# Expert 0 by its own 64 rows, the full sort behind it, one weight piece in the sorted rows' place and nine rotating buffers: a hybrid mixer and mixture-of-experts kernel

## The reference

```python
h = rmsnorm(x, norm1_g);  u = h @ w_in                     # 2048 -> 5632 columns
x = x + concat([conv(u_a), attention(u_q, u_k, u_v), conformer(u_c)]) @ w_out
h = rmsnorm(x, norm2_g)
pg = softmax(h @ rg_w + rg_b); grp = argmax(pg)            # 4 groups
le = (h @ re_w + re_b)[grp]                                # 8 experts in a group
q_top, e_top = top_k(softmax(le), 2)                       # 2 experts for each token
y[t] = sum over the 2 experts e:  gate * (silu(h[t] @ w_gate[e]) * (h[t] @ w_up[e])) @ w_down[e]
out = rmsnorm(x + y, final_g)
```

## Time and profile before

| | before |
|---|---|
| median of 3 runs | 1361.73 us |
| the profiled execution's own time | 1361.14 us |
| its span, first to last instruction | 1359.3 us |
| PE busy | 1235.7 us (91%) |
| DVE, ACT busy | 511.2, 280.0 us |
| DMA over the span | 471.8 MB, 347 GB/s |
| chain that ended last, by engine | PE 55%, DMA 40%, DVE 2% |

### The profile page before, as it was taken

One profiled execution on the slowest core, in us unless ns is written; L12 is line 12 of the kernel. 1 busy time (PEld: TensorE's weight loads), 2 busy tenths in 40 slices (PEclk: granted clock), 3 DMA queues, 4 the chain that ended last, 5 costly groups with the idle time before them and its releaser, 6 DMA issues.

```text
span 1359.3 us, 16672 instructions
## 1 busy us (share of the span) xinstructions
PE 1235.7 (91%) x6468; PEld 682.4 (50%) x6468; DVE 511.2 (38%) x906; ACT 280.0 (21%) x383; POOL 6.0 (0%) x27
## 2 busy tenths in 40 slices
PE   5999999989989999989899888989898989898896
PEld 5999999978866333333333333333333333333332
DVE  5365868655437422322222222222222222222224
ACT  5443444436343100100001000000100000100002
POOL 1000000000000000000000000000000000000000
PEclk9999999989999999999999999999999999999998
DMA  8555354547466999999999999999999999999994
GB/s 274 203 181 191 128 184 155 185 155 278 148 265 245 427 427 427 429 427 428 429 429 428 429 428 429 430 427 430 428 428 429 429 428 429 428 428 429 427 423 165
DMA packets 63443, 471.80 MB, mean 347 GB/s; under 512 B 5895, under 2 KB 6407, under 8 KB 37676
## 3 DMA queue, kind: packets, MB, share of 16 engines
q1 hardware_dynamic: 63404, 471.24, 84.5%
HBM read 469.13 MB, written 2.10 MB: 347 GB/s over the span
## 4 chain that ended last, share of the span: by engine, by line
PE 55%; DMA 40%; DVE 2%; issue 2%; ACT 1%; SPq 0%; DVEq 0%; ACTq 0%
DMA ring<-in_w_up 39%; PE bank L1301 24%; PE bank L1468 15%; PE bank L1503 8%; PE bank L1516 3%; PE bank L1445 1%; PE bank L1469 1%; DMA stage<-in_w_in 1%; PE bank L1485 1%; PE bank L1411 1%; PE bank L1478 0%; DVE x_tok L1174 0%; DVE zone_u L859 0%; ACT w_hi L354 0%; PE bank L1378 0%
## 5 line engine op out<-in xcount | busy, mean ns | idle before, releaser
L1468 PE MATMUL bank<-ring,win 128*64 128x512 f32 x992 | 442.9, 600 | 64.4 <-DMA ring<-in_w_up 64.4
L1469 PE MATMUL bank<-ring,win 128*64 128x512 f32 x992 | 443.8, 601 | 0.0
L1468 PEld LDWEIGHTS bank<-ring,win 128*64 128x64 f32 x992 | 132.3, 138 | 350.4 <-issue 315.8
L1174 DVE TENSOR_TENSOR x_tok<-x_tok,bank 128x512 f32<-128x512 f32 x256 | 158.7, 682 | 264.0 <-PE bank L1516 263.1
L1503 PE MATMUL bank<-ring,hiddenT 128*64 128x512 f32 x1024 | 226.8, 594 | 18.2 <-issue 17.5
L360 DVE TENSOR_TENSOR w_lo<-stage,w_hi 128x2048 fp32r<-128x2048 f32 x60 | 137.3, 2295 | 94.5 <-ACT w_hi L354 94.2
L1301 PE MATMUL bank<-h_hi,w_hi 128*128 128x256 f32 x576 | 163.7, 284 | 1.5 <-DVE w_lo L360 1.5
L1301 PE MATMUL bank<-h_lo,w_hi 128*128 128x256 f32 x576 | 163.3, 283 | 0.0
L1301 PE MATMUL bank<-h_hi,w_lo 128*128 128x256 f32 x576 | 163.3, 283 | 0.0
L1503 PEld LDWEIGHTS bank<-ring,hiddenT 128*64 128x64 f32 x1024 | 84.4, 137 | 136.7 <-issue 115.9
L354 ACT ACTIVATE w_hi<-stage 128x2048 fp32r<-128x2048 f32 x60 | 114.8, 1917 | 144.1 <-PE bank L1301 140.2
(11 more groups left out here) (222 smaller groups left out, 839.0 us busy)
## 6 DMA issues: line engine op xcount, KB each, us to landing
ring<-in_w_gate SPq DMA_DIRECT2D x62, 2048.0 KB, 27.0
ring<-in_w_up SPq DMA_DIRECT2D x62, 2048.0 KB, 31.1
ring<-in_w_down SPq DMA_DIRECT2D x62, 2048.0 KB, 27.1
stage<-in_w_in SPq DMA_DIRECT2D x44, 1024.0 KB, 4.9
stage<-in_w_out SPq DMA_DIRECT2D x16, 1024.0 KB, 5.1
ring<-in_w_up SPq DMA_DIRECT2D x4, 1024.0 KB, 16.8
ring<-in_w_gate SPq DMA_DIRECT2D x4, 1024.0 KB, 16.5
ring<-in_w_down SPq DMA_DIRECT2D x4, 1024.0 KB, 27.9
```

The lines of the kernel that those rows point to most:

```text
L1174: V.tensor_tensor(at, at, bank[banks[n]][:, :], ALU.add).then_inc(returned, 1)
L1468: M.matmul(bank[0][0:W_ROWS, :], rows_of[:, c, 0:W_ROWS], gate[:, at], start=(c == 0), stop=(c == C - 1))
L1469: ins = M.matmul(bank[0][UPPER, :], rows_of[:, c, 0:W_ROWS], up[:, at], start=(c == 0), stop=(c == C - 1))
```

## The change

1. The ring has nine buffers: seven from the start, the other two in the memory of y_hi and y_lo. Rounds are of three experts. silu_g and hidden share one tile, and final_w gets no memory of its own: it is loaded into ring buffer 7 after everything else.
2. Piece 2 goes to `zone_piece`, the first 4096 columns of zone_u, where x_sorted will stand later. So pieces 0 to 7 are issued before expert 0 is begun; piece 2 follows the loads of the third block of w_out.
3. ScalarE copies each block of x_tok into x_cols, channels regrouped (`columns_out`), two copies of 128x512 a block.
4. Expert 0's 64 rows come from a product of their own, x_cols with first_pick (a mask of 64 slots scaled by the norm), plain fp32, 32 matmuls of 64 columns; VectorE applies g2 and writes win.
5. h2_hi and h2_lo are made in four parts each from x_cols.
6. The sort is of all 512 slots, 16 chunks: chunks 0 to 2 before down(0), 3 to 15 behind it. Six banks rotate. ScalarE empties odd chunks, VectorE even ones. Expert 1's window waits for all.
7. SP's waits follow: pieces 8 and 9 after two quarters of expert 0, 10 after four, 11 and 12 behind down(0)'s halves, 13 and 14 behind half the sort and all of it (their memory held h2), 15 and 16 behind half of expert 1.

```diff
-RING = 8
-LATE = 7
-LATE_FROM = 4
-ROUND = 4
+RING = 9
+EARLY = 7
+FIRST_LOADS = EARLY + 1
+ZONE_PIECE = 2
+TURN = (0, 1, 2, 3, 4, 7, 8, 5, 6)
+ROUND = 3
 PIECE = C * NB // 2
 PART = PIECE // 2
-SORT = SLOTS // 2
+HC = C // 2
...
-        xT = u3(T * D, T, NB)
+        zone_piece = zone_u[:, 0:PIECE]
+        x_cols = u3(PIECE, T, D).rearrange("p t (c k) -> p t c k", c=C)
...
-        silu_g = sb("silu_g", [P, NB])
-        hidden = sb("hidden", [W_ROWS, NB])
+        rows_now = sb("rows_now", [P, NB])
+        silu_g, hidden = rows_now[W_ROWS:, :], rows_now[0:W_ROWS, :]
+        sq_out = (x_sorted_spare, rows_now[:, :])
+        win_t = sb("win", [P, C * W_ROWS])
+        win = win_t[:, :].rearrange("p (c n) -> p c n", c=C)
+        xT = win_t[:, :].rearrange("p (t n) -> p t n", t=T)
+        first_pick = sb("first_pick", [P, T, W_ROWS])
...
+        ring += [sb(f"ring{k}", [P, PIECE]) for k in range(EARLY, RING)]
+        final_w = ring[EARLY][:, 0:D]
...
+            assert n != ZONE_PIECE
+            if n < FIRST_LOADS:
+                return n - (n > ZONE_PIECE), 16
+            turn, at = divmod(n - FIRST_LOADS, RING)
+            slot = TURN[at]
+            return slot, 16 * (turn + 1 + (slot < EARLY))
...
-        SORT_BANK, SORT2_BANK = (0, 1, 2, 3, 6, 4, 5, 7), (1, 2, 3, 4, 5, 6, 7, 1)
+        WIN_BANK, SORT_BANK = (1, 2, 3, 6), (1, 3, 6, 7, 0, 2)
...
+                if b == 2:
+
+                    sp.wait_ge(yc_ready, J)
+                    sp.dma_start(zone_piece, first[gate_last]).then_inc(zone_loaded, 16)
...
+            load_piece(slot_of(0, up_last), first[up_last])
             sp.wait_ge(lo_made, chunk(LAST_OUT + 3))
-            load_piece(3, first_pieces[3])
+            load_piece(slot_of(0, down_first), first[down_first])
             sp.wait_ge(used, chunk(LAST_OUT + 2))
-            load_piece(4, first_pieces[4])
+            load_piece(slot_of(0, down_last), first[down_last])
             sp.wait_ge(used, chunk(LAST_OUT + 3))
-            load_piece(5, first_pieces[5])
-
-            gate_first, up_first, gate_last, up_last, down_first, down_last = range(PIECES)
-            second = expert_pieces(1)
             load_piece(slot_of(1, gate_first), second[gate_first])
-            for h in range(2):
-                for k, part in ((up_first, HALF[h]), (gate_last, HALF[h])):
-                    sp.wait_ge(in_used, h + 1)
-                    slot = slot_of(1, k)
-                    sp.dma_start(ring[slot][:, part], second[k][:, part]).then_inc(piece_loaded[slot], 16)
+            load_piece(slot_of(1, up_first), second[up_first])
...
+            sp.wait_ge(in_used, 2)
+            load_piece(slot_of(1, gate_last), second[gate_last])
+            load_piece(slot_of(1, up_last), second[up_last])
             sp.wait_ge(in_used, QUARTERS)
-            load_piece(slot_of(1, up_last), second[up_last])
             load_piece(slot_of(1, down_first), second[down_first])
-            sp.wait_ge(sorted2_done, 8)
+            sp.wait_ge(down_used, 2)
             load_piece(slot_of(1, down_last), second[down_last])
-            third = expert_pieces(2)
-            sp.wait_ge(down_used, 2)
+            sp.wait_ge(down_used, J)
             load_piece(slot_of(2, gate_first), third[gate_first])
-            sp.wait_ge(down_used, J)
+            sp.wait_ge(sorted_done, HC)
             load_piece(slot_of(2, up_first), third[up_first])
+            sp.wait_ge(sorted_done, C)
+            load_piece(slot_of(2, gate_last), third[gate_last])
             sp.wait_ge(in_used, QUARTERS + 2)
-            load_piece(slot_of(2, gate_last), third[gate_last])
-            for k in (up_last, down_first, down_last):
-                load_next(2, k, slot_of(2, k), third)
-            sp.dma_start(final_w[:, :], a["final_g"].rearrange("(o d) -> o d", o=1).broadcast_to([P, D])).then_inc(fg_loaded, 16)
-            fourth = expert_pieces(3)
-            for k in range(PIECES):
-                load_next(3, k, slot_of(3, k), fourth)
+            load_piece(slot_of(2, up_last), third[up_last])
+            load_piece(slot_of(2, down_first), third[down_first])
+            load_next(2, down_last, slot_of(2, down_last), third)
...
+            sp.dma_start(final_w, a["final_g"].rearrange("(o d) -> o d", o=1).broadcast_to([P, D])).then_inc(fg_loaded, 16)
...
+            def columns_out(b):
+
+                for t in range(T):
+                    act.wait_ge(mixed_added, 2 * b + t + 1)
+                    nc.scalar.activation(x_cols[:, t, :, b * NB // C:(b + 1) * NB // C],
+                                         x_tok[:, t, b * NB:(b + 1) * NB].rearrange("p (k c) -> p c k", c=C),
+                                         ACT.Copy).then_inc(x_cols_made, 1)
...
+            columns_out(BLOCKS - 1)
+            act.wait_ge(h_ready, T + 1)
+            act.wait_ge(used, chunk(4 * MOE_BLOCK0 - 1))
+            act.wait_ge(x_cols_made, T * BLOCKS)
+            for half in range(2):
+                for t in range(T):
+                    nc.scalar.activation(h2_half(0, t, half), x_cols[:, t, half * HC:(half + 1) * HC].rearrange("p c k -> p (c k)"),
+                                         ACT.Copy, scale=RSTD[:, t:t + 1]).then_inc(h2_hi_made, 1)
...
+            def sort_out(c):
+
+                act.wait_ge(sorted_done, c + 1)
+                nc.scalar.activation(x_sorted[:, c, :], bank[SORT_BANK[c % len(SORT_BANK)]][:, :], ACT.Copy,
+                                     scale=g2[:, c:c + 1]).then_inc(sorted_act, 1)
...
+            sort_out(1)
             act.wait_ge(down_used, J)
             nc.scalar.activation(y_rows[:, 0:NB], bank[4][:, :], ACT.Copy).then_inc(y_act, 1)
+            for c in range(3, C, 2):
+                sort_out(c)
+            act.wait_ge(starts_ready, 1)
+            act.wait_ge(sorted_act, HC)
+            act.wait_ge(sorted_dve, HC)
+            window(1)
...
+            V.tensor_tensor(FIRST_SLOT, SLOT[:, 0:T], SLOT[:, T:2 * T], ALU.min).then_inc(slot_first, 1)
+            dve.wait_ge(slot_first, 1)
+            for t in range(T):
+                V.tensor_scalar(first_pick[:, t, :], iota_row[:, 0:W_ROWS], FIRST_SLOT[:, t:t + 1], RSTD[:, t:t + 1],
+                                ALU.is_equal, ALU.mult).then_inc(first_picked, 1)
...
+            for i in range(C // WIN_C):
+                cs = slice(i * WIN_C, (i + 1) * WIN_C)
+                dve.wait_ge(first_rows, i + 1)
+                V.tensor_tensor(win[:, cs, :], bank[WIN_BANK[i]][:, 0:WIN_C * W_ROWS].rearrange("p (c n) -> p c n", c=WIN_C),
+                                g2[:, cs].unsqueeze(2).broadcast_to([P, WIN_C, W_ROWS]), ALU.mult).then_inc(first_win, 1)
...
+            for half in range(2):
+                for t in range(T):
+                    dve.wait_ge(h2_hi_made, T * half + t + 1)
+                    V.scalar_tensor_tensor(h2_half(1, t, half), x_cols[:, t, half * HC:(half + 1) * HC].rearrange("p c k -> p (c k)"),
+                                           RSTD[:, t:t + 1], h2_half(0, t, half).bitcast(F32),
+                                           ALU.mult, ALU.subtract).then_inc(h2_lo_made, 1)
...
+            crowded(0)
+            hidden_made(0)
+            sort_out(0)
+            hidden_back(0)
+            sort_out(2)
+            for i in range(1, 4):
                 crowded(i)
-            hidden_made(0)
-            for i in range(0, 8, 2):
-                evicted(sorted2_done, SECOND, SORT2_BANK, i, sorted2_dve)
-            hidden_back(0)
-            for i in range(OVER // 2, OVER):
+            upper_rows(0)
+            for c in range(4, C, 2):
+                sort_out(c)
+                if c in (6, 10):
+                    crowded(4 + (c == 10))
+            for i in range(6, OVER):
                 crowded(i)
             crowded_tables()
...
+            pe.wait_ge(x_cols_made, T * BLOCKS)
+            for t in range(T):
+                pe.wait_ge(first_picked, t + 1)
+            for c in range(C):
+                at = c % WIN_C * W_ROWS
                 for t in range(T):
-                    if p == 0:
-                        pe.wait_ge(pick_ready, t + 1)
-                        pe.wait_ge(h2_hi_made, t + 1)
-                    else:
-                        pe.wait_ge(h2_lo_made, t + 1)
-                    for i, b in enumerate(SORT_BANK):
-                        if p == 0 and t == 0 and b in (4, 5, 7):
-                            pe.wait_ge(places_saved, T + 1)
-                        for k in range(2):
-                            ins = sorted_from(bank[b][:, k * SORT:(k + 1) * SORT], part, t, 2 * i + k, slice(0, SORT),
-                                              p == 0 and t == 0 and k == 0, p == 1 and t == T - 1 and k == 1)
-                        if p == 1 and t == T - 1:
-                            ins.then_inc(sorted_done, 1)
+                    ins = M.matmul(bank[WIN_BANK[c // WIN_C]][:, at:at + W_ROWS], x_cols[:, t, c, :], first_pick[:, t, :],
```

(33 more changed lines are left out.)

## The result

The changed kernel takes 1366.49 us (median of 6 runs, 1365.47 to 1368.87), the kernel before 1361.27 in the runs beside it: ratio 1.0039, 95% interval [1.0029, 1.0049]. That is slower by 5.2 us. The prediction was 1367.6 with a range of 1360.0 to 1369.8. The profiled run took 1365.47 us with a span of 1363.7, 4.3 and 4.4 us over those of before.

The account below looks back on a forecast made before the run. From 424 us the weight stream was taken to bound the kernel. TensorE's steps from 407.6 summed to X = 470.4; X - 463.9 gave +6.5 us on the profiled 1361.14, so 1367.6, range 1360.0 to 1369.8.

Parts of the forecast that it names:

- first rival: Expert 0's 64-row product: the clock rises inside it, so it ends at 417.3; change +0.5 us, 1361.6; chance 27%.
- X: Moment when TensorE is half through expert 1 and SP can issue piece 15, the stream's last stop; forecast 470.4.
- Start of the product: Expert 0's new 64-row product on TensorE starts at about 407.6, where the sort started at 407.70.
- The product: Expert 0's 64 fp32 records on TensorE: 6.9 us at full clock, 13.7 at low; low taken, ending at 421.3.
- Gate and up: Expert 0's gate and up products: 13.9 us at full clock plus 2.0 for a cold start, done at 437.2.
- Turns, three chunks, down(0): Expert 0 behind gate and up: turns 1.0, three sorted chunks of 0.92, down 6.9; sum 10.7 us, to 447.9.
- Thirteen chunks: Rest of the sort behind down(0): 13 chunks of 0.92 us, 11.9, to 459.8, with evictions keeping up.
- Eviction, register, window: Between sort and expert 1: last eviction 0.8, ScalarE's register read 0.75, window 1.1, 0.1 to TensorE; to 462.5.
- Half of expert 1: Half of expert 1's gate and up: 7.1 us, plus 0.8 taken for the clock behind 2.7 us of idleness.
- form of the sum: Weight stream after its last stop: 4.92 us a piece before and after, so the change in time is X - 463.9.
- X - 463.9: Change in total time from X, at 4.92 us a piece of the weight stream; +6.5 us forecast.
- second hole: Weight stream between pieces 14 and 15: 0 GB/s for about 5 us, from 465.6 to 471.

Follow-up runs that it names:

- after_twice: Changed kernel with each of the 64-row product's 64 records issued once more, its result overwritten: 1379.10 us, ratio 1.0132 to the kernel before.
- after_128cols: Changed kernel with expert 0's product made 128 columns wide, the window taking the first 64: 1362.27 us, ratio 1.0004 to the kernel before.
- after_high_only: Changed kernel with expert 0's rows made from the high halves alone (fp32r, 32 records instead of 64): 1361.33 us, ratio 0.9998 to the kernel before.
- after_warm: Changed kernel with filling products, never read, in TensorE's waits around the routing to keep the clock up: 1359.77 us, ratio 0.999 to the kernel before.
- before_final_last: Kernel before with only the final norm's weights moved, issued behind the last expert's pieces: 1358.38 us, ratio 0.9982 to the kernel before.
- after_warm3b: Second run of the changed kernel with filling products around the routing, ahead of expert 1 and in the layer norm's idle stretch: 1354.75 us, ratio 0.9953.
- after_warm3: Changed kernel with filling products around the routing, ahead of expert 1 and ten in the layer norm's idle stretch: 1355.66 us, ratio 0.9959 to the kernel before.

## Why the prediction was right

The mechanism was the one predicted, and its steps can be read off one by one. The stated range alone would not have shown it, as it held the first rival's 1361.6 too; the product's 0.50 and the moment X do.

- *Start of the product:* 408.20 against 407.6; the routing ran 0.35 us later in this run, and the wait for the slots is 1.65.
- *The product:* 64 records at the low clock, 13.7 us expected, 13.8 from its start to expert 0's first product at 422.02. The choice between 6.9 and 13.7, the largest in the sum, fell right, but the reason given for it holds only in part. That the 40-column records were the nearer kind is borne out: behind the narrow records the clock did not rise in 27.5 us (after_twice). But their pace, which I put down to weight loads, is not what tells them apart: records of 128 columns keep the same pace, and behind 5.4 us of those it rose (after_128cols).
- *Gate and up:* 422.02 to 436.92, 14.9 us, of which 1.0 is the cold start; 2.0 was expected. The clock came back about 2 us into it (0.94 over 424 to 425), and not 4.
- *Turns, three chunks, down(0):* 436.92 to 447.91, 11.0 against 10.7. VectorE's gates were done at 432.9 (432.30 and 0.60), so it was hidden by 4 us and not 1.7: it made the low halves from contiguous rows, 4.9 us in two pairs, where I had taken the strided 7.56 of the earlier trace rows.
- *Thirteen chunks:* 12.0 against 11.9. The evictions kept up, 0.69 us on ScalarE and 0.75 on VectorE.
- *Eviction, register, window:* to 462.8, against 462.5.
- *Half of expert 1:* 7.1, and nothing for the idle stretch where I took 0.8. The bound of 0 to 1.6 was too narrow: it was 0 in the kernel after and after_twice, 1.7 in after_high_only and after_128cols, 3.0 in after_warm. And the reading that stretches of 1.94 us do no harm rested on one place. In the kernel after the clock fell behind one of 1.95 us (at 850.7), and in the kernel before behind three of 2.0 us later in the stream, here the first of them and a window of TensorE alone behind it, clock 0.50:

```profile
611.02 0.72 PE L1468 MATMUL bank<-ring,win 128*64 128x512 f32 x1 [2.02 <-DMA ring<-in_w_up]
...
612.00:613.00 1.00, 1.00 (x4) 0.50 0.97 410
```

X came out at 469.91, 0.5 under the forecast of 470.4. The misses (+0.6 for the start, -1.0, +0.3, -0.8 and tenths beside them) cancel in part, and that is luck. So is some of the time's agreement: 1367.6 was worked out for the profiled execution, and that took 1365.47, 2.1 less (0.5 of X, 1.6 of the form below); the median is 1.0 above it. The forecast's own range is also not what its bounds add up to: they give 1365.7 to 1369.3.

The Trainium skill (TensorE: Matmul & The Clock Gate, Part 1, The HAM clock gate) counts time of sustained activity, "not a number of matmuls". By that rule the product's clock would have risen, which was the first rival's 1361.6. after_128cols behaves so; after_twice, 27.5 us at 0.50 with no pause that the profile shows, doesn't, and there the measurement decides.

**The term that was mis-sized** is the form of the sum itself. X - 463.9 gives +6.0 for the measured X; expert 31's first product moved by 4.44. The form took 4.92 us a piece for both streams, which spreads the loss at a stream's start over all its pieces. Split at 4.90 a piece (428 GB/s) from where the DMA moves again, before: 1316.17 - 423.0 = 893.2 us for 181.5 pieces, of which 889.4 are the steady rate and 3.8 the start. After: 1320.61 - 470.8 = 849.8 for 173, 847.7 steady and 2.1 the start. The windows show a part of it, the first 20 us of the stream (kernel before; the kernel after's row of 471 to 491, 415 GB/s, stands above):

```profile
423.00:443.00 20.00, 19.29 (x120) 11.92 (x118) 11.94 (x56) 5.13 (x11) 0.00 (x0) 1.00 1.01 406
```

9 GB/s over 20 us is 0.4 us of the 1.7. The rest I can't place. It is not final_w: taking it out of the stream gave 2.1 us by the traces (before_final_last), less than the 2.45 of half a piece. Within the changed kernel the form holds: expert 31's first product starts at X + 850.7 to X + 851.0 in all eight profiles, over 23.8 us of X (459.29 in after_warm3b to 483.04 in after_twice).

The stream's second hole was 2.7 us (468.0 to 470.8) and not 5: piece 14 landed at 468.0 and not 465.6, 8 us behind its issue.

**The median.** The two medians are 5.2 apart, the two profiled runs 4.3. The difference, 0.9, is less than what single runs of one kernel differ by. The clock may have a hand in that: of the kernel after's six runs the three of 1365.5 to 1365.7 us have a mean clock of 0.986 to 0.987, the three of 1367.3 to 1368.9 one of 0.983 to 0.985. Where in the kernel they lost it isn't recorded, and that this is the cause isn't shown.

## What to carry to other kernels

When a stream of loads sets the end, find the last moment at which it stood still and what it waited for: each us of the work ahead of that moment is one at the end. Beyond it count only the bytes in the stream (half a piece was worth 2 to 3 us here) and the work behind the last arrival (a low clock there cost 1.7). A busy TensorE is not a warm one: before a product of narrow records is put behind an idle stretch, look at the granted clock there, and price it at both levels. And keep apart the parts of a change: here the moved sort and its product and all else but one load cost some 7.9 us, and the load issued last gave 2.7 of it back.

## What was not expected of the hardware

- A record of 64 columns takes 0.216 us at the low clock (13.8 / 64) and 0.113 at the high one (407.03 to expert 0's first product at 414.29, / 64); one of 128 columns takes the same, 0.213 and 0.112 from start to start. Doubling the columns made the product shorter, 9.98 against 13.89 us.
- Idle stretches of 1.9 to 2.8 us lowered the clock in some places and not in others. The same 2.75 us ahead of expert 1 did nothing in the kernel after and after_twice, and cost 1.7 us in after_high_only and after_128cols and 3.0 in after_warm. Later in the stream, 1.94 ahead of expert 31 did nothing in the kernel after, while 1.95 ahead of an earlier expert was followed by a fall (850.8); 2.20 and 2.10 were followed by 0.68 and 0.66 in the window 1310 to 1315 in after_warm3 and after_warm3b.
- The stream took time to come to its rate: 406 GB/s in its first 20 us before and 415 after, 428 later.
